# Expert weights in 4 MB transfers: four rows dealt per partition, and one place fewer ahead

## The chip, the cores and the metric

The kernel runs on one core of a Trainium2 chip. The metric is the device time of one execution in microseconds (us). The kernel before takes 1209.77 us, the median of 3 runs (1209.13 to 1209.91).

## What is computed

One layer of a hybrid decoder for 288 tokens (256 of a prompt, 8 x 4 of samples, width 1024, everything in float32). The front part is a projection of the normalised input into four parts, a gated linear recurrence and a pooling branch, a merge, and an output projection with a residual. The part that matters here is the mixture of 32 experts behind it, of which every token uses 4:

```python
def moe(u, w_router, b_router, w_gate_up, b_gate_up, w_down, b_down):
...
    for e in range(N_EXPERTS):
        gu = t @ w_gate_up[e] + b_gate_up[e]
        gate = jnp.minimum(gu[:, :D_EXPERT], SWIGLU_LIMIT)
        up = jnp.clip(gu[:, D_EXPERT:], -SWIGLU_LIMIT, SWIGLU_LIMIT)
        h = (up + 1.0) * (gate * jax.nn.sigmoid(SWIGLU_ALPHA * gate))
        out = out + comb[:, e:e + 1] * (h @ w_down[e] + b_down[e])
```

`w_gate_up[e]` is 1024 x 2048 and `w_down[e]` 1024 x 1024, so an expert has 12 MB (12,582,912 bytes) of weights, and the 32 experts 403 MB, each read once. A tail follows: the embedding of the layer, gated by a projection with `w_ple_gate` (4 MB), and a last norm.

## The kernel before

**Pieces.** The weights of an expert come in six pieces of 2 MB: four of gate and up (`w_gate_up`), each of 256 channels (rows of the matrix), and two of `w_down`, each of 512 rows. A piece lies over 128 partitions with 16 KB in each. For gate and up partition p holds the rows 2p and 2p+1 of its 256 (`k=2` in `expert_piece`, L661), 8 KB each and neighbours in memory; for down it holds the rows 4p to 4p+3 of its 512. So each partition is one run of 16 KB. In SBUF a piece is four blocks of 1024 values.

**Order.** Experts go in pairs, m = 0 to 15, and pairs in quads of 24 pieces (`STREAM`, L94). Within a pair the order is: gate and up of the even expert (4 pieces), of the odd one (4), down of the even one (2), of the odd one (2). Pieces are numbered 0 to 191 here.

**Places.** The ring has eight places (`SLOTS`), in which pieces follow one another. Beside them are two extra places, made of buffers that other stages have left. `AHEAD = {8: 0, 9: 1, 18: 1, 27: 1, 36: 1}` says which pieces lie in one of these: piece 8 in the first, and 9, 18, 27 and 36 one after another in the second, which is called the ninth place here. `held_before` (L132) tells which piece held the place of piece n before. An extra place is filled by two transfers, of 1.5 and 0.5 MB.

**SP** issues all weight transfers, in order: before each one it waits until the piece that held the place has been used (`opening_piece`, L694, for the first two quads; `quad_pieces`, L673, in a loop for five quads and once more for the last quad; `ring_place_used`, L655). Its transfers run one behind another on the same 16 DMA engines. The last piece comes as two halves, so that PE can start on the first. Behind it SP loads `w_ple_gate` in four transfers of 1 MB (L751), which need two ring places.

**PE** (`quad`, L1267) does for a pair: bias products for gate and up (`begin_sums`, L1178), 4 x 16 matmuls of 512 columns (`weigh_gate_up`, L1201), the sums of the pair before (`add_pair`, L1236), gate and up of the odd expert, the turned hidden rows (`turn_hidden`, L1168), down of both (`weigh_down`, L1222, 16 matmuls for each piece), and the gathered tokens of the next pair (`gather`, L1076 and L1083). Expert products have 64 token rows, and two of them run at once on two halves of the array: half g makes the output columns 512g to 512g+511. PE waits for a piece in `wait_expert_piece` (L494), and after its last matmul raises the semaphore on which SP waits.

**Tokens.** `x_tok` holds the normalised token rows in order. The gather reads them with a step of two (`x_blocks`, `"p (j c k) -> p j k c"`, k=2), so that the gathered channels lie as the rows of a gate-and-up piece do, and VectorE scales them by `gain_pairs` when it takes them (`gathered`, L2094).

**ScalarE** (`quad`, L1638) does the sigmoid, the copies out of PSUM, and, in pair 0, `copy_residual` (L1606), which copies two token tiles to where the sums are kept. **GpSimd** loads small things; `p_sample` (L817) goes into memory that the ninth place uses, so it waits until piece 36 is used.

## Time and profile before

| | |
|---|---|
| median of 3 runs | 1209.77 us (1209.13 to 1209.91) |
| profiled execution: time, span | 1210.05 us, 1208.3 us |
| PE busy | 1169.4 us (97%) |
| VectorE, ScalarE, GpSimd busy | 27%, 18%, 2% |
| mean granted TensorE clock | 0.996 |
| read from HBM | 444.51 MB, 369 GB/s over the span |
| SP's DMA queue | 440.04 MB in 50512 packets |

The span runs from the first instruction to the last one; the execution's own time is 1.75 us longer. PE's 97% is time in which some matmul was in flight, and that of the expert stage contains two at once. GB/s in a window of the page is what all 16 DMA engines moved. The page's slices are 30.2 us long.

### The profile page before, as it was taken

The page shows a single profiled execution, that of the slowest core. Times are in us where ns is not written, and L with a number is a line of the kernel's source. Part 1 is how long each engine was busy: PE and PEld are TensorE (multiplying, and loading weights), DVE is VectorE, ACT ScalarE, POOL GpSimd, SP SyncE. Part 2 cuts the span into 40 slices and gives each one's busy share as a digit, 9 for nine tenths or more (in the row PEclk, how much of TensorE's full clock was granted, in tenths as well). Part 3 has the DMA queues.
Part 4 walks back from the last instruction along what each step waited for, and adds up shares of the span by engine and source line. Part 5 has one row for each costly group of instructions (what it writes and reads, how often), then busy time and mean ns, then how long its engine had stood idle before and what let it go on. Part 6 is the DMA issues. An engine that isn't in the chain of part 4 may idle for free.

```text
span 1208.3 us, 14638 instructions
## 1 busy us (share of the span) xinstructions
PE 1169.4 (97%) x5836; PEld 553.0 (46%) x5836; DVE 331.4 (27%) x864; ACT 213.7 (18%) x420; POOL 29.2 (2%) x64
## 2 busy tenths in 40 slices
PE   9999999999999999999989899999998999799997
PEld 7777777443443434343333333434434343334344
DVE  4844214250322222131312120313222212111223
ACT  2556302112010101101010112120101010101034
POOL 2001000000000000000000020000000000000000
PEclk9999999999999999999999999999999999999999
DMA  9935573679999999999999999999999999999961
GB/s 287 360 141 203 173 279 133 237 283 429 427 428 426 427 426 428 427 427 429 427 428 428 427 428 425 429 427 426 430 426 428 427 428 430 425 428 428 426 260 40
DMA packets 53287, 446.82 MB, mean 370 GB/s; under 512 B 8174, under 2 KB 11470, under 8 KB 28424
## 3 DMA queue, kind: packets, MB, share of 16 engines
q1 hardware_dynamic: 50512, 440.04, 87.8%
q0 software_dynamic: 2464, 5.71, 1.6%
q8 instruction: 40, 0.66, 0.2%
q10 hardware_dynamic: 256, 0.30, 0.1%
q14 instruction: 15, 0.12, 0.0%
HBM read 444.51 MB, written 1.88 MB: 369 GB/s over the span
## 4 chain that ended last, share of the span: by engine, by line
PE 78%; DMA 20%; ACT 1%; DVE 1%; issue 1%; SPq 0%; DVEq 0%
PE ps L1201 31%; PE ps L864 16%; DMA ring<-in_w_gate_up 14%; PE ps L1222 11%; PE ps L1236 4%; PE ps L1083 3%; DMA ring<-in_w_down 3%; DMA ring<-in_w_ple_gate 2%; PE ps L1016 2%; PE ps L1355 2%; PE ps L1178 2%; PE ps L1168 1%; PE ps L898 1%; PE ps L858 1%; PE ps L885 1%; PE ps L1076 1%
## 5 line engine op out<-in xcount | busy, mean ns | idle before, releaser
L1201 PE MATMUL ps<-ring,work 128*64 128x512 f32 x2000 | 443.6, 597 | 2.8 <-DMA ring<-in_w_gate_up 2.6
L1201 PEld LDWEIGHTS ps<-ring,work 128*64 128x64 f32 x2000 | 141.2, 138 | 273.6 <-issue 261.9
L1222 PE MATMUL ps<-ring,work 128*64 128x512 f32 x992 | 223.4, 595 | 19.4 <-DMA ring<-in_w_down 19.4
L864 PE MATMUL ps<-work,ring 128*128 128x288 f32 x736 | 180.6, 407 | 0.0
L864 PEld LDWEIGHTS ps<-work,ring 128*128 128x128 f32 x736 | 139.7, 190 | 39.6 <-issue 1.7
L1222 PEld LDWEIGHTS ps<-ring,work 128*64 128x64 f32 x992 | 70.6, 137 | 146.8 <-issue 127.6
L2122 DVE TENSOR_SCALAR work<-ps 128x512 f32<-128x512 f32 x32 | 22.1, 691 | 374.5 <-PE ps L1201 374.5
L2094 DVE TENSOR_TENSOR work<-ps,gain_pairs 128x256 f32<-128x256 f32 x60 | 25.5, 424 | 286.2 <-PE ps L1083 286.2
L1626 ACT ACTIVATE work<-work 128x512 f32<-128x512 f32 x32 | 20.2, 631 | 442.9 <-DVE work L2122 442.9
L1083 PE MATMUL ps<-work,x_tok 128*128 128x128 f32 x512 | 65.4, 285 | 0.0
L1083 PEld LDWEIGHTS ps<-work,x_tok 128*128 128x128 f32 x512 | 61.8, 197 | 3.9 <-issue 2.0
L1236 PE MATMUL ps<-work 128*128 128x512 f32 x128 | 59.2, 606 | 1.4 <-DVE stat L1944 1.4
L1570 ACT COPY work<-ps 128x512 f32<-128x512 f32 x32 | 18.7, 585 | 196.1 <-PE ps L1168 196.1
L1635 ACT COPY work<-ps 64x512 f32<-64x512 f32 x31 | 17.9, 578 | 152.5 <-PE ps L1222 152.5
L2105 DVE TENSOR_TENSOR u_tok<-u_tok,ps 128x512 f32<-128x512 f32 x64 | 40.8, 680 | 2.5 <-PE ps L1236 2.5
L1236 PEld LDWEIGHTS ps<-work 128*128 128x128 f32 x128 | 23.0, 190 | 31.0 <-issue 29.1
L1168 PEld LDWEIGHTS ps<-ident,work 128*128 128x128 f32 x128 | 17.9, 209 | 26.0 <-issue 26.0
L1016 PE MATMUL ps<-ring,work 128*128 128x512 f32 x64 | 28.9, 600 | 0.0
L1355 PE MATMUL ps<-ring 128*128 128x512 f32 (+1 forms) x80 | 28.3, 511 | 0.3 <-DMA ring<-in_w_ple_gate 0.3
L1178 PE MATMUL ps<-work,pick_gu 96*64 96x512 bf16 x128 | 20.6, 399 | 4.8 <-issue 4.4
L1168 PE MATMUL ps<-ident,work 128*128 128x128 f32 x128 | 23.9, 310 | 0.0
L2124 DVE TENSOR_SCALAR work<-ps 128x512 f32<-128x512 f32 x32 | 22.1, 691 | 5.3 <-PE ps L1201 5.3
(286 smaller groups left out, 663.0 us busy)
## 6 DMA issues: line engine op xcount, KB each, us to landing
ring<-in_w_gate_up SPq DMA_DIRECT2D x125, 2048.0 KB, 29.5
ring<-in_w_down SPq DMA_DIRECT2D x61, 2048.0 KB, 29.6
ring<-in_w_in SPq DMA_DIRECT2D x7, 2048.0 KB, 19.0
work<-in_w_gate_up SPq DMA_DIRECT2D x3, 1536.0 KB, 12.9
ring<-in_w_proj_b SPq DMA_DIRECT2D x2, 2048.0 KB, 10.0
ring<-in_w_proj_a SPq DMA_DIRECT2D x2, 2048.0 KB, 10.1
ring<-in_w_out SPq DMA_DIRECT2D x2, 2048.0 KB, 9.4
ring<-in_w_ple_gate SPq DMA_DIRECT2D x4, 1024.0 KB, 28.6
```

Source lines behind the costliest of these rows:

```text
L864: mm = pe.matmul(out(b), lhs, rhs, start=(k == 0), stop=(k == len(pairs) - 1))
L1016: mm = pe.matmul(ps[0:ROWS[t], b, :], out_rows[t][k], out_weights[half][k], start=(k == 0), stop=(k == KC - 1))
L1083: mm = pe.matmul(ps[:, B_X[q], k * P:k * P + P], x_blocks[t][:, q, k, :], sel[t], start=False, stop=(last and k == 1))
L1168: mm = pe.transpose(ps[:, b, j * P:j * P + P], block, ident[:])
L1178: pe.matmul(ps[half(g), b, :], pick[0:BIAS_ROWS, :], bias_parts[0:BIAS_ROWS, at + 512 * g:at + 512 * g + 512], start=True, stop=False)
L1201: mm = pe.matmul(ps[half(g), b, :], xg[:, k, i % 2, :], blocks[2 * (k % 2) + at][:, 512 * g:512 * g + 512], start=False, stop=(k == KC - 1))
L1222: mm = pe.matmul(ps[half(g), b, :], hT_of[i % 2][:, 4 * j + k, :], blocks[k][:, 512 * g:512 * g + 512], start=False, stop=(4 * j + k == KC ...
L1236: mm = pe.matmul(ps[:, bank, :], sel_wT[:, t, :], o_pair[:, 512 * h:512 * h + 512], start=True, stop=True)
L1355: mm = pe.matmul(ps[:, b, 0:c1 - c0], x2T[:, k, tok(t)], gate_rows(k, c0, c1), start=(k == 0), stop=(k == KC - 1))
L2094: V.tensor_tensor(xg[:, own, :, :], ps[:, b, 0:2 * P].rearrange("p (c i s) -> p c i s", c=2, i=2), gains, ALU.mult).then_inc(emptied[b], 1)
L2105: V.tensor_tensor(x_half, x_half, ps[:, bank, 0:own.stop - own.start], ALU.add) \
L2122: V.tensor_scalar(gate, ps[:, b, :], LIMIT, None, ALU.min).then_inc(emptied[b], 1)
```

## The change

It has five parts.

1. From piece 20 on (`JOINED = 20`), SP joins two pieces that follow one another in `STREAM` (two of gate and up, or the two of down) into one transfer of 4 MB, which fills two ring places. Its source is 512 rows of gate and up, four to a partition (`RUN = 4`), or all 1024 rows of down, eight to a partition: one run of 32 KB each. It is issued when the second of the two places is free. PE waits for both pieces on one semaphore. Pieces 0 to 19 stay transfers of 2 MB. The last two pieces (190, 191) also stay apart, and 191 stays in halves. That makes 85 transfers of 4 MB.
2. `AHEAD` becomes `{8: 0, 9: 1}`: the ninth place holds piece 9 alone, and 18, 27 and 36 go into the ring. The ring then turns in pairs of places.
3. Gate and up rows lie in fours from pair 2 on, so the gathered channels have to as well. ScalarE rewrites the token tiles once, in pair 1 (`deal_inputs`): two copies of 128 x 1024 and eight small ones of 32 x 128. From pair 2 on the gather reads these rows, now without a step, and the gains come from a second table (`gain_fours`), which GpSimd loads.
4. Down rows lie in eights. So half g of the array now makes the output columns 8c+4g to 8c+4g+3 of gate and up, for all c: each gate and up matmul, and its bias product, reads its moving operand as 128 groups of four values with a step of eight (`dealt`), where it read 512 values in a row. This holds for all pairs.
5. GpSimd no longer waits for piece 36 before it loads `p_sample`.

```diff
+RUN = 4
+
+JOINED = 20
+
+DEALT_PARTS = 10
...
-AHEAD = {8: 0, 9: 1, 18: 1, 27: 1, 36: 1}
+AHEAD = {8: 0, 9: 1}
...
+        def two_pieces(q):
+
+            return ring[:, MOE_SLOT[q]:MOE_SLOT[q] + 2, :, :].rearrange("p s a b -> p (s a b)")
+
+        def dealt(row, g):
+
+            return row.rearrange("p (c g k) -> p c g k", g=2, k=RUN)[:, :, g, :]
+
+        def in_fours(m):
+
+            return not (isinstance(m, int) and m < 2)
...
-            eng.wait_ge(piece_landed[s], turn * 16 + 16)
+            at = STREAM.index((i, q))
+            first, turn = (s, turn) if isinstance(Q, int) and Q * QUAD_PIECES + at < JOINED else \
+                place(Q, *STREAM[at // 2 * 2])
+            eng.wait_ge(piece_landed[first], turn * 16 + 16)
...
-            def expert_piece(r, q, e, in_halves=False):
+            def expert_rows(q, e):
 
                 if q < GU_PIECES:
-                    src = gu_rows[bass.ds(e * D + 2 * P * q, 2 * P), :].rearrange("(p k) c -> p (k c)", k=2)
-                else:
-                    src = dn_rows[bass.ds(e * D + 4 * P * (q - GU_PIECES), 4 * P), :] \
-                        .rearrange("(p k) c -> p (k c)", k=4)
-                if in_halves:
-                    sp.dma_start(whole_piece(r)[:, 0:2 * D], src[:, 0:2 * D]).then_inc(last_half_landed, 16)
-                    sp.dma_start(whole_piece(r)[:, 2 * D:4 * D], src[:, 2 * D:4 * D]).then_inc(piece_landed[r], 16)
-                    return
-                sp.dma_start(whole_piece(r), src).then_inc(piece_landed[r], 16)
+                    return gu_rows[bass.ds(e * D + RUN * P * (q // 2), RUN * P), :] \
+                        .rearrange("(p k) c -> p (k c)", k=RUN)
+                return dn_rows[bass.ds(e * D, D), :].rearrange("(p k) c -> p (k c)", k=2 * RUN)
+
+            def piece_half(q):
+
+                return slice(RUN * D * (q % 2), RUN * D * (q % 2) + RUN * D)
 
             def quad_pieces(quads, e0, last=False):
 
-                for at in range(QUAD_PIECES):
-                    ring_place_used(quads, at)
+                for at in range(0, QUAD_PIECES, 2):
                     i, q = STREAM[at]
-                    expert_piece((at - EXTRAS) % SLOTS, q, e0 + i, last and at == QUAD_PIECES - 1)
+                    r = (at - EXTRAS) % SLOTS
+                    if last and at == QUAD_PIECES - 2:
+                        ring_place_used(quads, at)
+                        sp.dma_start(whole_piece(r), expert_rows(q, e0 + i)[:, piece_half(q)]) \
+                            .then_inc(piece_landed[r], 16)
+                        ring_place_used(quads, at + 1)
+                        place_, src = whole_piece((r + 1) % SLOTS), expert_rows(q + 1, e0 + i)[:, piece_half(q + 1)]
+                        sp.dma_start(place_[:, 0:2 * D], src[:, 0:2 * D]).then_inc(last_half_landed, 16)
+                        sp.dma_start(place_[:, 2 * D:4 * D], src[:, 2 * D:4 * D]).then_inc(last_landed, 16)
+                        continue
+                    ring_place_used(quads, at + 1)
+                    sp.dma_start(two_pieces(r), expert_rows(q, e0 + i)).then_inc(piece_landed[r], 16)
...
             def opening_piece(n):
 
-                later, at = divmod(held_before(n), QUAD_PIECES)
+                later, at = divmod(held_before(n if n < JOINED else n + 1), QUAD_PIECES)
                 i, q = STREAM[at]
                 piece_used(i, q, later)
-                if n in AHEAD:
-                    three, one = extra_parts[AHEAD[n]]
-                    extra_rows(n, 0, three)
-                    extra_rows(n, 3, one)
+                r = ring_turn(n) % SLOTS
+                if n < JOINED:
+                    sp.dma_start(whole_piece(r), piece_rows(n)).then_inc(piece_landed[r], 16)
                     return
                 later, at = divmod(n, QUAD_PIECES)
                 i, q = STREAM[at]
-                expert_piece(ring_turn(n) % SLOTS, q, 4 * later + i)
+                sp.dma_start(two_pieces(r), expert_rows(q, 4 * later + i)).then_inc(piece_landed[r], 16)
...
-            for n in range(SLOTS + 2, OPENING * QUAD_PIECES):
+            for n in list(range(SLOTS + EXTRAS, JOINED)) + list(range(JOINED, OPENING * QUAD_PIECES, 2)):
...
-            quads, at = divmod(max(AHEAD), QUAD_PIECES)
-            i, q = STREAM[at]
-            pool.wait_ge(piece_used_up[q], 4 * quads + i + 1)
...
+            x_fours = [x_tok[:, t, :].rearrange("p (j k c) -> p j k c", c=P, k=2) for t in range(TT - 1)]
...
-                gather_samples()
+                if isinstance(m, int) and m == 2:
+                    pe.wait_ge(x1_dealt, DEALT_PARTS)
+                gather_samples(in_fours(m))
                 for q in range(QUARTERS):
                     for t in TILES[1:]:
-                        gather_tile(q, t)
+                        gather_tile(q, t, in_fours(m))
...
+                    row = bias_parts[0:BIAS_ROWS, at:at + D]
                     pe.matmul(ps[half(g), b, :], pick[0:BIAS_ROWS, :],
-                              bias_parts[0:BIAS_ROWS, at + 512 * g:at + 512 * g + 512],
+                              row[:, 512 * g:512 * g + 512] if kind == "out" else dealt(row, g),
...
                             mm = pe.matmul(ps[half(g), b, :], xg[:, k, i % 2, :],
-                                           blocks[2 * (k % 2) + at][:, 512 * g:512 * g + 512],
+                                           dealt(blocks[2 * (k % 2) + at], g),
...
+            def deal_inputs():
+
+                for b in B_X:
+                    act.wait_ge(filled[b], inputs_gathered(b, 1, False))
+                for t in range(2):
+                    act.wait_ge(x1_copied, t + 1)
+                    nc.scalar.copy(x_tok[:, t, :].rearrange("p (j k c) -> p j k c", k=RUN, c=P),
+                                   x2[t].rearrange("p (j c k) -> p j k c", k=RUN, c=P)).then_inc(x1_dealt, 1)
+                act.wait_ge(comb_ready, 1)
+                src = flat_x[:, 2 * D:2 * D + QW].rearrange("p (c g k) -> p g k c", g=2, k=2)
+                for j in range(2):
+                    for g in range(2):
+                        for h in range(2):
+                            nc.scalar.copy(sample_fours[own_quarter(2 * j + g), :, 64 * h:64 * h + 64],
+                                           src[own_quarter(2 * j + h), g, :, :]).then_inc(x1_dealt, 1)
```

**How it moves the instructions.** SP, the transfers behind pieces 8 and 9; the first row is pieces 10 and 11. Before (L671 is the ring, L692 the ninth place):

```order
L671 DMA ring<-in_w_down 128x4096 x2
L671 DMA ring<-in_w_gate_up 128x4096 x6
L692 DMA work<-in_w_gate_up 128x3072
L692 DMA work<-in_w_gate_up 128x1024
L671 DMA ring<-in_w_gate_up 128x4096
L671 DMA ring<-in_w_down 128x4096 x4
L671 DMA ring<-in_w_gate_up 128x4096 x3
L692 DMA work<-in_w_gate_up 128x3072
L692 DMA work<-in_w_gate_up 128x1024
L671 DMA ring<-in_w_gate_up 128x4096 x4
```

And now (L748 is a transfer of 2 MB, L752 one of 4 MB; 4096 and 8192 are values per partition):

```order
L748 DMA ring<-in_w_down 128x4096 x2
L748 DMA ring<-in_w_gate_up 128x4096 x8
L752 DMA ring<-in_w_down 128x8192 x2
L752 DMA ring<-in_w_gate_up 128x8192 x4
L752 DMA ring<-in_w_down 128x8192 x2
L752 DMA ring<-in_w_gate_up 128x8192 x4
L752 DMA ring<-in_w_down 128x8192 x2
```

Before, the pieces 18, 27 and 36 went to the ninth place in two transfers each. Now 18 is the last but one of the single transfers, and from piece 20 on each transfer carries two pieces.

SP, the end of the program. Before (L668 and L669 are the halves of piece 191, L751 is `w_ple_gate`):

```order
L671 DMA ring<-in_w_down 128x4096 x3
L537 ISA
L668 DMA ring<-in_w_down 128x2048
L669 DMA ring<-in_w_down 128x2048
L652 ISA
L751 DMA ring<-in_w_ple_gate 128x2x1024 x4
```

And now (L703 is piece 190, L707 and L708 are the halves of 191):

```order
L711 DMA ring<-in_w_down 128x8192
L703 DMA ring<-in_w_down 128x4096
L562 ISA
L707 DMA ring<-in_w_down 128x2048
L708 DMA ring<-in_w_down 128x2048
L677 ISA
L781 DMA ring<-in_w_ple_gate 128x2x1024 x4
```

Pieces 188 and 189 were transfers of their own and are one now (L711); 190 and the halves of 191 stay.

ScalarE, the end of pair 0 and the begin of pair 1, now (L1641 is `copy_residual`, L1649 and L1656 are `deal_inputs`, L1677 is the sigmoid of pair 1):

```order
L1641 COPY u_tok<-x_tok 128x1024 x2
L1686 COPY work<-ps 64x512
L1687 COPY work<-ps 64x512
L1649 COPY x_tok<-u_tok 128x1024 x2
L1656 COPY x_tok<-x_tok 32x2x64 x8
L1677 ACTIVATE work<-work 128x512
```

Before, the sigmoid followed the two copies of `keep_output` (now L1686, L1687) at once.

## Rows read from the trace of the kernel before

**Rows 1.** The page, 40 slices of the span: DMA busy tenths and rate.

```profile
DMA  9935573679999999999999999999999999999961
GB/s 287 360 141 203 173 279 133 237 283 429 427 428 426 427 426 428 427 427 429 427 428 428 427 428 425 429 427 426 430 426 428 427 428 430 425 428 428 426 260 40
```

**Rows 2.** Windows, two stretches: busy us of each engine, granted clock, DMA share, GB/s.

```profile
core 0: us, PE busy (x) PEld busy (x) DVE busy (x) ACT busy (x) POOL busy (x), PEclk, DMA share, GB/s
60.00:70.00 10.00, 10.00 (x45) 7.29 (x44) 0.48 (x1) 8.22 (x18) 0.00 (x0) 1.00 1.05 387
400.00:500.00 100.00, 100.00 (x524) 39.82 (x522) 23.56 (x63) 9.24 (x16) 0.51 (x1) 1.00 1.01 427
```

**Rows 3.** DMA, 60 to 70 us: packets; issues with KB each and us to landing.

```profile
DMA packets 1919, 3.87 MB, mean 387 GB/s; under 512 B 31, under 2 KB 31, under 8 KB 1919
...
ring<-in_w_proj_b SPq DMA_DIRECT2D x1, 2048.0 KB, 12.2
```

**Rows 4.** DMA, 400 to 500 us, the same columns.

```profile
DMA packets 2957, 42.67 MB, mean 427 GB/s; under 512 B 339, under 2 KB 339, under 8 KB 355
...
ring<-in_w_gate_up SPq DMA_DIRECT2D x13, 2048.0 KB, 23.8
```

**Rows 5.** The chain that ended last: start us, us, what.

```profile
355.18 3.97 PE ps L1083 x32
359.69 13.73 PE ps L1201 x64
...
413.55 13.73 PE ps L1201 x64
...
554.50 32.79 DMA ring<-in_w_gate_up
...
669.51 35.27 DMA ring<-in_w_gate_up
...
1168.86 14.02 PE ps L1355 x32
```

**Rows 6.** Waits of the whole span, PE: us in total, times, longest.

```profile
PE ps L1222 <- DMA ring<-in_w_down: 19.4, 24, 1.2
...
PEld ps L1222 <- DMA ring<-in_w_down: 16.6, 13, 2.0
```

**Rows 7.** Timeline of SP: start us, us, transfers x count, pieces 19 to 23.

```profile
297.25 0.33 SPq L671 DMA_DIRECT2D ring<-in_w_gate_up  x1
300.68 15.83 SPq L671 DMA_DIRECT2D ring<-in_w_down  x4
```

**Rows 8.** Timeline of SP, one row: piece 22.

```profile
312.75 0.33 SPq L671 DMA_DIRECT2D ring<-in_w_down  x1
```

**Rows 9.** DMA, the one transfer issued at 297.25: us to landing.

```profile
ring<-in_w_gate_up SPq DMA_DIRECT2D x1, 2048.0 KB, 13.7
```

**Rows 10.** Source line L671, all 2 MB transfers: us from issue to landing.

```profile
DMA to landing us min/median/max: 7.7/29.6/36.1
```

**Rows 11.** Timeline of PE at the end of pair 15: start us, us, what [idle before].

```profile
1143.57 3.65 PE L1222 MATMUL ps<-ring,work 128*64 128x512 f32 x16 [0.40 <-DMA ring<-in_w_down]
...
1148.37 3.65 PE L1222 MATMUL ps<-ring,work 128*64 128x512 f32 x16 [0.47 <-DMA ring<-in_w_down]
...
1153.94 7.09 PE L1222 MATMUL ps<-ring,work 128*64 128x512 f32 x32 [1.10 <-DMA ring<-in_w_down]
...
1168.13 0.38 PE L904 MATMUL ps<-stat,fold 128*128 128x1 f32 x2
1168.86 6.71 PE L1355 MATMUL ps<-ring 128*128 128x512 f32 x15 [0.34 <-DMA ring<-in_w_ple_gate]
```

**Rows 12.** Groups of weight loads by form, whole span: busy us, mean ns.

```profile
L1083 PEld LDWEIGHTS ps<-work,x_tok 128*128 128x128 f32 x512 | 61.8, 197 | 3.9 <-issue 2.0
L1236 PEld LDWEIGHTS ps<-work 128*128 128x128 f32 x128 | 23.0, 190 | 31.0 <-issue 29.1 <-DVE stat L1944 1.9
L1168 PEld LDWEIGHTS ps<-ident,work 128*128 128x128 f32 x128 | 17.9, 209 | 26.0 <-issue 26.0
```

**Rows 13.** Groups of PE, pair 2 (359.53 to 413.38 us): busy us, mean ns.

```profile
L1201 PE MATMUL ps<-ring,work 128*64 128x512 f32 x112 | 24.6, 593 | 0.0
```

**Rows 14.** Timeline of ScalarE around pair 1.

```profile
294.57 1.99 ACT L1606 COPY u_tok<-x_tok 128x1024 f32<-128x1024 f32 x2
...
301.27 0.58 ACT L1636 COPY work<-ps 64x512 f32<-64x512 f32 x1
319.49 0.63 ACT L1626 ACTIVATE work<-work 128x512 f32<-128x512 f32 x1 [17.64 <-DVE work L2122]
```

**Rows 15.** Timeline of PE: the gather for pair 1.

```profile
301.25 4.04 PE L1083 MATMUL ps<-work,x_tok 128*128 128x128 f32 x32
```

**Rows 16.** Timeline of GpSimd: start us, us, what [idle before].

```profile
116.97 0.79 POOL L806 DMA_DIRECT2D gain_pairs<-in_g_moe  x1
130.61 0.51 POOL L810 DMA_DIRECT2D u_tok<-in_b_gate_up  x1 [12.85 <-ACT work L1458]
```

More of the change, by code:

```diff
@@ L435, in hybrid_layer @@
         x1_copied = sem("x1_copied")
+        x1_dealt = sem("x1_dealt")
         sel_w_ready = sem("sel_w_ready")
@@ L684, in piece_rows @@
                 e = 4 * quads + i
-                if q < GU_PIECES:
+                if q < GU_PIECES and not in_fours(n // (QUAD_PIECES // 2)):
                     return w_gate_up[0, e, 2 * P * q:2 * P * q + 2 * P, :].rearrange("(p k) c -> p (k c)", k=2)
-                rows = 4 * P * (q - GU_PIECES)
-                return w_down[0, e, rows:rows + 4 * P, :].rearrange("(p k) c -> p (k c)", k=4)
+                return expert_rows(q, e)[:, piece_half(q)]
             def extra_rows(n, k, dst):
@@ L807, in _ @@
                            g_moe[0].rearrange("(j p k) -> p j k", p=P, k=2)).then_inc(gain_landed, 16)
+            pool.dma_start(gain_fours[:].rearrange("p (j k) -> p j k", k=RUN),
+                           g_moe[0].rearrange("(j p k) -> p j k", p=P, k=RUN)).then_inc(gain_landed, 16)
             pool.wait_ge(ya_ready, PG)
@@ L1067, in _, with gather_samples @@
             turn_residual(1, 0)
-            x_blocks = [x_tok[:, t, :].rearrange("p (j c k) -> p j k c", c=P, k=2) for t in range(TT - 1)]
-            def gather_samples():
+            x_pairs = [x_tok[:, t, :].rearrange("p (j c k) -> p j k c", c=P, k=2) for t in range(TT - 1)]
+            x_fours = [x_tok[:, t, :].rearrange("p (j k c) -> p j k c", c=P, k=2) for t in range(TT - 1)]
+            def gather_samples(fours=False):
+                rows = sample_fours if fours else sample_rows
                 for k in range(2):
@@ L1075, in gather_samples, with gather_tile @@
                         own = own_quarter(q)
-                        pe.matmul(ps[:, b, k * P:k * P + P], sample_rows[own, k, :], sel[TT - 1][own, :],
+                        pe.matmul(ps[:, b, k * P:k * P + P], rows[own, k, :], sel[TT - 1][own, :],
                                   start=(k == 0), stop=False)
-            def gather_tile(q, t):
+            def gather_tile(q, t, fours=False):
                 last = t == TILES[-1]
+                x_blocks = x_fours if fours else x_pairs
                 for k in range(2):
@@ L1643, in quad @@
                         embedding_squares()
+                    if begins and j == 1:
+                        deal_inputs()
                     swish(m, 0)
@@ L2048, in _ @@
             b = turns["rank"][0]
-            dve.wait_ge(gain_landed, 16)
+            dve.wait_ge(gain_landed, 16 * 2)
             def take_inputs(q):
@@ L2092, in gathered @@
                     own = slice(2 * j, 2 * j + 2)
-                    gains = gain_pairs[:, own].unsqueeze(2).unsqueeze(3).to_broadcast([P, 2, 2, CAP])
+                    gains = (gain_fours if in_fours(m) else gain_pairs)[:, own].unsqueeze(2).unsqueeze(3) \
+                        .to_broadcast([P, 2, 2, CAP])
                     V.tensor_tensor(xg[:, own, :, :], ps[:, b, 0:2 * P].rearrange("p (c i s) -> p c i s", c=2, i=2), gains,
@@ L2158, in quad @@
                             dve.wait_ge(x1_copied, 2)
+                            dve.wait_ge(x1_dealt, 2)
                             dve.wait_ge(row_copied, 1)
```

10 lines of the change are left out of this document (6 added, 4 removed).

## The prediction

> **What bounds the kernel now.** I read the 40 slices first. From the tenth slice to the 38th the DMA engines are full and move 425 to 430 GB/s [rows 1]. Before it, in the front part, they are not full, so nothing that the change does there counts. Next I compared what the two sides need for one pair of experts. PE started gate and up of one pair at 359.69 us and of the next at 413.55, with no wait between: 53.86 us [rows 5]. A pair has 12 pieces, 25.17 MB, and at 427 GB/s [rows 2] that is 58.9 us. So DMA is the slower side by 5 us in a pair. PE begins with pieces in stock, and from about 554 us on it waits: the chain of waits then runs through transfers of weights (32.79 us at once at 554.50, 35.27 at 669.51) [rows 5], and PE waited for down pieces 19.4 and 16.6 us in total [rows 6]. These 36 us are all that PE has to spare. Last comes the end. PE waited 0.40, 0.47 and 1.10 us for pieces 188, 189 and 190, then 0.34 us for the last quarter of `w_ple_gate`, and began the last projection at 1168.86 [rows 11]. So two rules hold. A microsecond of the DMA stream after about 260 us is a microsecond of the kernel, whether it is a faster run or an idle queue. And at the very end PE is only 0.34 us from being the last itself.
>
> **The change, part by part.**
>
> *Longer runs, gain.* The cost of a run comes from two stretches with full engines. At 60 to 70 us the runs are of 2 KB (512 columns of a matrix; 1919 packets for 3.87 MB) and the rate is 387 GB/s; at 400 to 500 us they are of 16 KB and it is 427 [rows 2 to 4]. An engine has a sixteenth of that: 84.7 ns for 2048 B, 613.9 ns for 16384 B. The line through both is 36.9 ns for each 1000 bytes and 9.1 ns fixed per run. A run of 32 KB then takes 1218.6 ns instead of 1227.8. A 4 MB transfer has 8 such runs on each engine, which saves 8 x 9.1 = 73 ns, and there is one completion packet fewer per engine (339 small packets in 100 us are about 16 for each of 20 transfers [rows 4]), taken at the same 9 ns. Together 82 ns, and with 85 transfers 7.0 us. Bounds: the line could be steeper at its foot, or a run of 32 KB could be cut in two. Then only the completions are saved, 0.8 us. On the other side the rate cannot exceed the line's slope, 433.5 GB/s, which is 146 ns per transfer or 12.4 us. I take 7.0, since the straight line is all that the two rows support.
>
> The Trainium skill (SBUF — State Buffer, "The DMA setup-cost knee") has 2 us fixed per transfer and 436 GB/s behind it, so 4 MB in one would take 2 us less than in two, 170 us in all. The trace disagrees for transfers that queue: those of 2 MB already move at 427 GB/s.
>
> *The ninth place and the joined wait, loss.* This is what decides. In the trace before, SP issued piece 19 at 297.25, 20 at 300.68, 21, 22 and 23 behind it, with 22 at 312.75 [rows 7, 8]. Each time is the moment when PE had used the piece that held the place (9 for 18, 10 for 19, 11 for 20, 12 for 21, 13 for 22). Without the refill of the ninth place everything moves back by one: 18 takes the place of 10 (297.25), 19 that of 11 (300.68), 20 that of 12 and 21 that of 13. And 20 and 21 are the first joined transfer, so both wait for piece 13, until 312.75. The stock in the queue doesn't last so long. Piece 19 was issued at 297.25 and landed 13.7 us later, at 310.9 [rows 9]; it lands then in the change too, as 18 and 19 are still issued before the engines run dry (each piece takes 4.9 us). In an empty queue a transfer of 2 MB takes at least 7.7 us from issue to landing [rows 10], 2.8 us over its 4.9. So the first byte of 20 effectively flows at 315.5, where it would have followed at 310.9: the DMA engines idle for 4.6 us, or about 5.8 if the start of an empty queue takes as much as a typical one of that stretch. I take 5.0. Once is enough: 22 and 23 wait for piece 15 and 24 and 25 for 17, both freed in time, and after that PE, with 53.86 us a pair, frees places faster than DMA fills them. Nothing gives those 5.0 us back, since the engines are full from there to the end.
>
> *No refills of the ninth place.* Three refills came as two transfers with runs of 12 and 4 KB: per engine 8 runs and a completion more, 82 ns, times three. Gain 0.25 us.
>
> Up to here the stream is shifted by 5.0 - 0.25 - 7.0 = -2.25 us at its end.
>
> *Waiting for both pieces.* In the middle this costs nothing, for PE uses two pieces in 7 to 9 us and a landing comes every 9.7. At the end it does. Before, 188 could start at 1143.57, while 189 landed for 1148.37 [rows 11]. Now both start when 189 has landed, at 1148.37 - 2.25 = 1146.1. From the start of 188 to that of 189 PE needs 4.80 - 0.47 = 4.33 us, and from there to 190 5.57 - 1.10 = 4.47 [rows 11]. So 190 starts at 1154.9, not 1153.94: 1.0 us later, although the stream is earlier. PE is ready for the last projection at 1168.51 + 1.0 = 1169.5, `w_ple_gate` has landed at 1168.86 - 2.25 = 1166.6, and PE becomes the last: 1169.5 against 1168.86 is **+0.65 us**.
>
> *Dealt reads on PE.* No row shows a moving operand with a step. The nearest are weight loads of 128 x 128: 190 ns in a row, 197 ns at every second value, 209 ns at every fourth [rows 12]. The lower end is 0 (or a gain, if a row in pieces were quicker; nothing suggests it). The upper end takes the 19 ns of 128 values that each open a new 16 bytes: a matmul reads 128 groups, so +19 ns on 593 [rows 13], 3%, and up to four times that if each value suffers as in a weight load. I take 0, because a group of four float32 fills 16 bytes, and the reads in a row open a new 16 bytes as often.
>
> The rule behind this is in the Trainium skill (SBUF — State Buffer, "Door 1: The DMA port swizzle"): SBUF has lines of 16 bytes and going to a new one costs. By it the dealt read costs nothing. The weight loads above agree in direction; no row here shows the dealt read itself.
>
> *ScalarE's dealing.* Two copies like those of L1606 (1.99 us) and eight small ones, 4 us in all. They start when pair 1's tokens are gathered, at 305.3 [rows 15], and ScalarE's next work is at 319.49 [rows 14]: hidden. The first reader of the dealt rows is the gather at 355.18 [rows 5]. The gather itself then loads without a step, 190 instead of 197 ns; PE has the spare time anyway, 0. GpSimd's added load stands ahead of the bias loads, where GpSimd waits 12.85 us for other work and one load takes it 0.8 us [rows 16]: 0. Its dropped wait frees only a small load that nobody waits for: 0.
>
> **Sum.** 1210.05 + 0.65 = 1210.7 us for the profiled execution. The median of the runs is 0.28 less, so **1210.4 us**: no change. About 0.2%, 2.4 us, is what a measurement can tell from none.
>
> **Rivals.**
>
> *A. Dealt reads slow PE.* For: the weight loads do pay for a step. Against: 16 bytes stay together. Gate and up are eight pieces of 3.43 us in a pair (13.73 for four [rows 5]), 27.5 us. At +10% a pair needs 2.75 us more, 16 pairs 44 us, which is 8 over the 36 that PE has to spare: 1218. It decides from some 4% on, as the spare time isn't spread evenly, and at 5% it is about +3: 1213. Slower. Chance 0.15.
>
> *B. The change doesn't do what it says: a 32 KB run goes as two packets.* Then the shift is 5.0 - 0.25 - 0.8 = +3.95, 190 starts at 1148.37 + 3.95 + 8.8 = 1161.1, and the end is +6.9: 1216.6. Nothing in the trace has such a run, for or against. Chance 0.07.
>
> *C. The rate rises more than the line says.* At the line's slope, 433.5 GB/s, 12.4 us instead of 7.0: shift -7.65, and 190 starts at 1149.5, the end is -4.8: 1205.0. For: part of the fixed cost may belong to the transfer, not to the run. Against: the line. Chance 0.10. Chance 0.12. The Trainium skill (DMA: Bandwidth & Descriptors, "Where 436 GB/s comes from") has 435 GB/s as the ceiling; at that the saving would be 15.4 us and the time 1202.
>
> *D. The queue doesn't run dry at 310.9*, because PE frees 13 earlier: 5.0 us less, 1205.4. Against: PE was never waiting there, so it has nothing to be earlier by. Chance 0.03.
>
> *E. Something else costs PE a few us near the end,* where it has just become the last: longer packets ahead of its code, a lower granted clock after longer waits. +1 to +4, say 1212.5. Chance 0.09.
>
> The forecast itself has 0.56. Its own range is 1208.6 to 1213.2: the saving between 5 and 8.6 us, the idle queue between 4.6 and 5.8.
>
> **Numbers.** Faster: C and D, 0.13. Slower: B 0.07, most of A 0.12, most of E 0.07, together 0.26. The rest, 0.61, is the same. The range goes up to take in B and ends at 1216.8; it leaves out C and D (0.13) and the far end of A (0.05), and begins at 1206.5, which takes in a C of half the size.
>
> **What the new profile would show.** The rate in the windows from 400 us on: 430 to 431 GB/s (427: B, 433: C), with some 1,300 packets over 8 KB in 100 us instead of 2,602. A gap in DMA at about 309 to 315, with SP's first 128x8192 issue at 312.75. Gate and up matmuls at 593 ns and 13.73 us for 64 (more: A). At the end a wait of PE for pieces 188 and 189 together, none for `w_ple_gate`. I am wrong if the gap isn't there, or if the rate lies outside 429 to 432.

## The result, and the profile after

The changed kernel takes **1228.14 us** (median of 4 runs, 1227.73 to 1228.84) beside 1209.45 us (4 runs, 1209.13 to 1209.91) for the kernel before: a ratio of 1.0156, 95% interval 1.0144 to 1.0168. It is 18.7 us slower. The forecast was 1210.4 us, in a range that ended at 1216.8. (Where a line number in the text above differs by a few lines from the printed listing, the listing is right. Below, line numbers are those of each kernel's own file.)

The page of the changed kernel, profiled at 1228.20 us:

```profile
span 1226.5 us, 14434 instructions
...
PE   9999999999999999998989996799999999799997
...
DMA  9936563589899999999999999599999999999951
GB/s 288 374 115 223 183 272 132 223 331 420 362 427 430 432 434 428 429 432 431 433 430 433 431 432 430 230 396 437 431 427 431 434 433 430 430 431 431 423 215 39
DMA packets 40647, 446.82 MB, mean 364 GB/s; under 512 B 6798, under 2 KB 10094, under 8 KB 26664
...
q1 hardware_dynamic: 37840, 440.03, 85.9%
```

Beside the same row for the kernel before [rows 1] one sees three things. The rate in the full stretches went from 427 to some 431 GB/s. The 11th slice, at 307 to 337 us, is at 362. And the 26th slice, at 767 to 797 us, is at 230. Nothing in the prediction speaks of that last one. Windows of the changed kernel around the places:

```profile
core 0: us, PE busy (x) PEld busy (x) DVE busy (x) ACT busy (x) POOL busy (x), PEclk, DMA share, GB/s
...
300.00:320.00 20.00, 20.00 (x126) 9.50 (x127) 6.40 (x22) 8.94 (x13) 0.00 (x0) 1.00 0.79 325
...
400.00:500.00 100.00, 99.52 (x522) 38.95 (x520) 24.55 (x65) 9.77 (x17) 0.00 (x0) 1.00 1.00 431
```

```profile
755.00:760.00 5.00, 0.00 (x0) 0.00 (x0) 0.00 (x0) 0.00 (x0) 0.00 (x0) 0.67 0.98 419
...
770.00:775.00 5.00, 1.55 (x16) 0.60 (x16) 0.00 (x0) 2.05 (x4) 0.00 (x0) 0.50 0.40 173
775.00:780.00 5.00, 5.00 (x24) 1.64 (x22) 0.00 (x0) 0.37 (x1) 0.00 (x0) 0.79 0.00 0
780.00:785.00 5.00, 5.00 (x42) 2.32 (x39) 0.00 (x0) 1.44 (x3) 0.00 (x0) 1.00 0.29 79
```

First PE stands still with all engines (755 to 760), while DMA works on. Then the DMA engines run dry (770 to 785). The chain that ended last says who holds whom:

```profile
719.39 2.02 ACT work L1617 x4
721.41 0.65 ACT tails L1620 x3
722.06 0.09 issue
722.15 9.67 POOL out L862 x19
731.82 40.98 DMA out<-work
772.79 0.02 issue
772.82 0.59 ACT work L1600
773.41 0.04 issue
773.45 1.94 PE ps L927 x16
```

The 40.98 us are neither weights nor any transfer that the change touches. GpSimd issues 20 stores of the recurrent state (16 of `conv_sample` and `pool_sample`, and four more) in pair 8. The tile `ple`, into which ScalarE next copies the embedding (`keep_embedding`, L1589 before), lies on the memory of that state (`state_z`), so ScalarE waits until all stores have landed. PE waits for ScalarE, frees no ring place, SP cannot issue, and the queue runs dry. The same places before and now, first the kernel before (timelines of GpSimd and ScalarE; issues with KB each and us to landing):

```profile
717.56 10.19 POOL L833 DMA_DIRECT2D out<-work  x20 [299.76 <-ACT tails L1585]
...
747.26 1.56 ACT L1565 COPY work<-ps 128x512 f32<-128x512 f32 x3 [3.19 <-DMA out<-work]
...
out<-work POOLq DMA_DIRECT2D x9, 12.0 KB, 12.0
out<-work POOLq DMA_DIRECT2D x8, 16.0 KB, 13.2
```

The changed kernel, with PE's wait and SP's four issues of this stretch (the last one is at 783.67, 39 us behind the third):

```profile
722.15 10.19 POOL L862 DMA_DIRECT2D out<-work  x20 [428.58 <-ACT tails L1620]
...
772.82 2.05 ACT L1600 COPY work<-ps 128x512 f32<-128x512 f32 x4 [24.14 <-DMA out<-work]
...
PE ps L927 <- ACT work L1600: 19.1, 1, 19.1
...
729.74 54.26 SPq L711 DMA_DIRECT2D ring<-in_w_gate_up  x4
...
out<-work POOLq DMA_DIRECT2D x9, 12.0 KB, 24.7
out<-work POOLq DMA_DIRECT2D x8, 16.0 KB, 27.6
```

The stores take GpSimd the same 10.19 us to issue, and twice as long to land: 24.7 and 27.6 us instead of 12.0 and 13.2. ScalarE waited 3.19 us before and 24.14 now. PE waited 19.10 us, so its own work covered about 5.0 of ScalarE's 24.14. By that estimate the chain was, before, only some 1.8 us (5.0 - 3.19) short of showing on PE.

Why twice as long? The stores are 640 packets on GpSimd's queue in both kernels, 40 for each of the 16 engines; 542 of them have 4 bytes. Their packets (queue q0: count, MB, share of the 16 engines' time) in two stretches, 715 to 735 and 735 to 760 us, of the kernel before:

```profile
q0 software_dynamic: 384, 0.21, 3.5%
...
q0 software_dynamic: 256, 0.13, 1.7%
```

and the changed kernel, the same stretches (715 to 735, 735 to 760 us) and a third, 760 to 775:

```profile
q0 software_dynamic: 133, 0.11, 1.7%
...
q0 software_dynamic: 351, 0.16, 2.2%
...
q0 software_dynamic: 156, 0.07, 1.7%
```

The records of single packets name no engine, but the order shows in them: behind 573 of the 640 packets before, and 584 of the 640 now, a packet of weights starts within 5 ns of its end. I read that as turns: an engine does one packet of GpSimd's queue, then one of SP's, and so on. SP's packet was 16 KB and 0.61 us; now it is 32 KB and 1.22 us. 40 turns are 24.6 us before and 48.7 us now; in the records the 640 packets run from 721.2 to 746.8 us and from 725.9 to 772.4. The Trainium skill (DMA: Bandwidth & Descriptors, "Queues, rings and completion order") says that an engine takes turns between the rows of its queues, a packet at a time, with some 9 to 17 descriptors in a packet. The trace agrees on the turns; on SP's side a turn is here a single run of a partition, 16 or 32 KB, and its length is what the other queue pays.

**Where the 18.2 us are** (the difference of the two profiled spans). PE starts the last projection at 1187.03 us (1168.86 before [rows 11]). The bytes that SP's queue has moved by a time, in pieces of 2 MiB, split it (a piece takes 4.88 us):

| us | before | after | difference | in us | cause |
|---|---|---|---|---|---|
| 340 | 41.67 | 40.74 | -0.93 | -4.5 | idle queue at 310 |
| 720 | 119.00 | 118.78 | -0.22 | +3.5 | longer runs |
| 850 | 145.26 | 141.87 | -3.39 | -15.5 | the stores |
| 1150 | 206.34 | 203.43 | -2.91 | +2.3 | longer runs |

(The causes are assigned by what lies in each stretch; the experiments below try them one by one.) The stream is 14.2 us late at the end. The other 4.0 us are PE's, in the last pair (timeline of the changed kernel; before: [rows 11]):

```profile
1162.17 5.35 PE L1257 MATMUL ps<-ring,work 128*64 128x512 f32 x16 [2.51 <-DMA ring<-in_w_down]
...
1168.13 3.65 PE L1257 MATMUL ps<-ring,work 128*64 128x512 f32 x16
...
1172.44 7.03 PE L1257 MATMUL ps<-ring,work 128*64 128x512 f32 x32
...
1187.03 13.97 PE L1390 MATMUL ps<-ring 128*128 128x512 f32 x32
```

PE waits once, 2.51 us, for 188 and 189 together, and the 16 matmuls after it take 5.35 us instead of 3.65: the granted clock stood at half, 1.2 GHz, for 3.4 us from 1162.8 on. Before, it had waited 0.40 and 0.47 us there and kept the clock.

### The profile page after: what moved, and what is told of

It reads as the page before. It is cut to its first block, busy times and chain, and to the rows that moved or that the text cites. A ratio compares the mean times of both kernels' runs of the same rounds, so it can differ in the third digit from the quotient of the medians.

```text
span 1226.5 us, 14434 instructions
## 1 busy us (share of the span) xinstructions
PE 1167.6 (95%) x5836; PEld 550.9 (45%) x5836; DVE 331.5 (27%) x864; ACT 220.8 (18%) x430; POOL 29.9 (2%) x65
## 4 chain that ended last, share of the span: by engine, by line
PE 76%; DMA 21%; ACT 1%; DVE 1%; POOL 1%; issue 1%; SPq 0%; DVEq 0%; ACTq 0%
PE ps L1236 28%; PE ps L893 16%; PE ps L1257 13%; DMA ring<-in_w_down 10%; DMA ring<-in_w_gate_up 8%; PE ps L1115 4%; PE ps L1271 4%; DMA out<-work 3%; PE ps L1045 2%; PE ps L1390 2%; PE ps L1213 2%; PE ps L1202 1%; PE ps L927 1%; POOL out L862 1%; PE ps L1107 1%; PE ps L914 1%
## 5 line engine op out<-in xcount | busy, mean ns | idle before, releaser
L1236 PE MATMUL ps<-ring,work 128*64 128x512 f32 x2048 | 451.8, 595 | 3.4 <-DMA ring<-in_w_gate_up 3.3
L1236 PEld LDWEIGHTS ps<-ring,work 128*64 128x64 f32 x2048 | 145.2, 137 | 278.9 <-issue 265.8
L1257 PE MATMUL ps<-ring,work 128*64 128x512 f32 x992 | 226.1, 604 | 19.6 <-DMA ring<-in_w_down 19.6
L1257 PEld LDWEIGHTS ps<-ring,work 128*64 128x64 f32 x992 | 71.7, 139 | 148.2 <-issue 141.5
L2148 DVE TENSOR_TENSOR work<-ps,gain_fours 128x256 f32<-128x256 f32 x56 | 23.8, 425 | 286.8 <-PE ps L1115 286.8
L1677 ACT ACTIVATE work<-work 128x512 f32<-128x512 f32 x32 | 20.2, 631 | 428.1 <-DVE work L2176 428.1
L1115 PE MATMUL ps<-work,x_tok 128*128 128x128 f32 x512 | 62.6, 280 | 0.0
L1115 PEld LDWEIGHTS ps<-work,x_tok 128*128 128x128 f32 x512 | 59.0, 192 | 3.9 <-issue 2.1
L1605 ACT COPY work<-ps 128x512 f32<-128x512 f32 x32 | 18.7, 585 | 209.0 <-PE ps L1202 209.0
L1686 ACT COPY work<-ps 64x512 f32<-64x512 f32 x31 | 17.9, 578 | 143.8 <-PE ps L1257 143.8
L1213 PE MATMUL ps<-work,pick_gu 96*64 96x512 bf16 x128 | 21.2, 408 | 5.0 <-issue 4.7
```

The costliest lines, as they stand in the source:

```text
L1115: mm = pe.matmul(ps[:, B_X[q], k * P:k * P + P], x_blocks[t][:, q, k, :], sel[t], start=False, stop=(last and k == 1))
L1213: pe.matmul(ps[half(g), b, :], pick[0:BIAS_ROWS, :], row[:, 512 * g:512 * g + 512] if kind == "out" else dealt(row, g), start=True, stop=F ...
L1236: mm = pe.matmul(ps[half(g), b, :], xg[:, k, i % 2, :], dealt(blocks[2 * (k % 2) + at], g), start=False, stop=(k == KC - 1))
L1257: mm = pe.matmul(ps[half(g), b, :], hT_of[i % 2][:, 4 * j + k, :], blocks[k][:, 512 * g:512 * g + 512], start=False, stop=(4 * j + k == KC ...
L2148: V.tensor_tensor(xg[:, own, :, :], ps[:, b, 0:2 * P].rearrange("p (c i s) -> p c i s", c=2, i=2), gains, ALU.mult).then_inc(emptied[b], 1)
```

## The experiments

Theory S: small stores take turns with long packets, and this is the loss. Rivals: something else in the change holds pair 8 (the dealt rows, the joined waits), or the early gap and the tail weigh more than thought. Each ratio is to the kernel before in the same session (1209.42 to 1209.48 us).

**Runs of 16 KB, the rest of the change kept.**

```diff
-                    sp.dma_start(two_pieces(r), expert_rows(q, e0 + i)).then_inc(piece_landed[r], 16)
+                    both_pieces(r, expert_rows(q, e0 + i))
```

`both_pieces` issues the two halves of each partition's run as two transfers of 2 MB, one behind the other, at the same moment; PE still waits for both.

> The changed kernel, but each 4 MB transfer is issued as two of 2 MB right behind one another, with runs of 16 KB. Places, waits for places and PE's wait for both pieces stay. Theory (each small packet of the state stores on GpSimd's queue waits for one weight packet on its DMA engine, and these are twice as long now): the stores land some 26 us after the first issue instead of 50, PE's 19 us wait in the embedding and the idle DMA behind it go, and what stays is the idle queue at 309 us and the late end: 1216. The rate is back at 427 GB/s. Rival (the joined waits and the missing ninth place themselves make the embedding late): the wait stays, 1228.

Measured: 1219.14 us, ratio 1.0079 (1.0062 to 1.0095). The stall is gone: ScalarE waits for no store, and the stores land in 11.8 and 13.1 us. The rate is 427 GB/s again. But 3 us more are lost than expected: at 1150 us its stream is 0.94 pieces, 4.6 us, behind that of the kernel before, and its last projection starts 9.0 us later (1177.84), so 4.4 us lie in the last pair.

**Eleven stores instead of 20, the rest of the change kept.** The 16 stores of the samples go by row of the window instead of by sample:

```diff
-            for b in range(DB):
-                at = 16 + DS * b
-                stores += [(conv_sample[0, b], state_z[at + 1:at + DS, 0, :]),
-                           (pool_sample[0, b, PB - DS:PB, :], state_z[at:at + DS, 1, :])]
+            for i in range(DS):
+                own = slice(16 + i, 16 + DS * DB, DS)
+                stores += [(pool_sample[0, :, PB - DS + i, :], state_z[own, 1, :])]
+                if i:
+                    stores += [(conv_sample[0, :, i - 1, :], state_z[own, 0, :])]
```

> The changed kernel, but the 16 stores of sample state are made as 7, one for each token position over all 8 samples: 11 store transfers instead of 20 for the same bytes. Theory: 22 packets per engine instead of 40, at 1.2 us each about 27 us, the wait goes nearly whole: 1210 (my first forecast was 1210.4). Rival (it isn't the number of small packets; the bytes or the weight stream decide): 1228.

Measured: **1211.08 us**, ratio 1.0017 (1.0007 to 1.0027). This edit alone gives back 17.1 of the 18.7 us. Its trace has 352 packets for the stores, 22 per engine, and

```profile
722.25 5.60 POOL L863 DMA_DIRECT2D out<-work  x11 [428.60 <-ACT tails L1621]
...
752.45 1.56 ACT L1601 COPY work<-ps 128x512 f32<-128x512 f32 x3 [3.67 <-DMA out<-work]
```

with no wait of PE. (The profiled execution took 1213.71 us, near the top of its runs.)

**JOINED = 24**, four more pieces in transfers of their own.

> The changed kernel, but joined from piece 24 on (20 to 23 stay single, so 20 waits for piece 12 only). Theory: of the 4.2 us in which DMA idles at 309 us 3 go, all else stays: 1225. Rival (that gap is no loss, because the stall in the embedding covers it): 1228.

Measured: 1228.02 us, ratio 1.0150 (1.0133 to 1.0167): a miss. The gap at 310 shrinks (DMA share 0.93 from 300 to 320), but 24 and 25 now wait for piece 17, until 331.55, and a second gap opens there (0.89 from 320 to 340). At 340 us the stream stands at 40.74 pieces, as in the changed kernel: the gap was moved, not removed. So the prediction's "freed in time" for pieces 24 and 25 holds only behind a gap that has already been paid. The stall in pair 8 is there as in the changed kernel. As the gap stayed, the run doesn't decide its rival, that the gap costs nothing beside the stall.

**The kernel before with more stores**: each of its 16 sample stores in two, 36 transfers in all, weights in 16 KB runs.

```diff
+            stores = stores[:4] + [(dst[k], src[k]) for dst, src in stores[4:] for k in (slice(0, 2), slice(2, None))]
```

> The kernel before, with its runs of 16 KB, but each of the 16 stores of sample state is made as two: 36 store transfers instead of 20. Theory: 72 packets per engine instead of 40, each behind a weight packet of 0.61 us, so they land some 45 us after the first issue, as in the changed kernel: PE waits some 19 us in the embedding, and the time rises by 12 to 18 us to 1222 to 1228. Rival (the run length alone, or the joined waits, make the stall): 1209.5.

Measured: 1216.33 us, ratio 1.0059 (1.0042 to 1.0076). Nothing of the change is in this kernel, and it has the stall:

```profile
764.85 2.05 ACT L1566 COPY work<-ps 128x512 f32<-128x512 f32 x4 [20.84 <-DMA out<-work]
...
PE ps L899 <- ACT work L1566: 12.8, 1, 12.8
```

The time is less than expected (1222 to 1228): PE's wait was 12.8 us instead of 19.1, the DMA engines idled some 3.5 us, and the stream lost 6.8 us between 720 and 850 us instead of 15.5. That the ring refills here place by place, and in the changed kernel two places at a time, may have its part in this; no run shows it alone. The four kernels by one rule, packets per engine times SP's packet:

| kernel | store packets per engine | SP's packet | product | first store issued to ScalarE's copy |
|---|---|---|---|---|
| before | 40 | 0.61 us | 24.6 us | 29.7 us |
| seven stores | 22 | 1.22 us | 26.8 us | 30.2 us |
| before, stores halved | 72 | 0.61 us | 44.2 us | 47.7 us |
| changed | 40 | 1.22 us | 48.7 us | 50.7 us |

The product orders all four and leaves 2 to 5 us for the issue. With the three edits above (shorter packets or fewer stores take the stall away, more stores bring it into the kernel before), that settles S.

**What the rest of the change is worth.** With the seven stores: 188 and 189 apart again.

```diff
+                    if last and at == QUAD_PIECES - 4:
+                        for h, landed_ in enumerate((piece_landed[r], even_landed)):
+                            ring_place_used(quads, at + h)
+                            sp.dma_start(whole_piece(r + h), expert_rows(q, e0 + i)[:, piece_half(q + h)]) \
+                                .then_inc(landed_, 16)
+                        continue
```

> The changed kernel with 7 stores of sample state (the second experiment, 1211.1), and pieces 188 and 189 as transfers of their own. Theory (at the end PE waits 2.5 us for the joined 188 and 189, and behind that wait runs 3.4 us at half clock): both go, and since the weight stream of that run was 2.1 us ahead of that of the kernel before at 1150 us, the time is 1207.5. Rival (the end is set by the stream, not by the joined wait): 1211.

Measured: 1209.63 us, ratio 1.0000 (0.9991 to 1.0009), 1.4 us less than without the edit by the medians, 2.1 by the ratios (expected 3.6). In its profiled execution (1210.94 us) PE waits for no transfer from 1040 us on, so an earlier stream has nothing more to give there.

With the seven stores and JOINED = 36 (transfers of 4 MB from the second quad's middle on):

> The changed kernel with 7 stores, joined from piece 36 on. Theory (joining costs a gap where the queue's stock is short of one piece; at 36 the stock has grown enough, while from 24 the gap only moved to 330 us): no gap in DMA after 260 us, 4.5 us less than 1211.1: 1206.6. Rival (a gap comes at whatever piece joining begins): 1211.

Measured: 1209.56 us, ratio 0.9998 (0.9989 to 1.0007), 1.5 us less than with JOINED = 20, where 4.5 were expected. The DMA share from 300 to 320 us is 0.94, so a part of the gap is left.

With all three:

> Both edits together, with 7 stores: theory 1203, the longer runs' gain without the gap, the late end and the stall. If the gain of the runs were smaller than 7 us: 1206 or more.

Measured: **1207.0 us**, ratio 0.9976 (0.9967 to 0.9985). It beats both kernels, by 2.5 and 21 us, and is 4 us short of what was expected.

Two things explain the shortfall. The first, 1.8 us, is what the ninth place was worth, tried on the kernel before with `AHEAD = {8: 0, 9: 1}` and GpSimd's wait for piece 36 taken out, nothing joined:

> The kernel before, in which only the ninth place is filled once (pieces 18, 27 and 36 go into the ring), with nothing joined. Theory (the gap comes from the missing place and the joined wait together; alone the missing place delays piece 20 only until 309.3): a gap of about 1 us at 309 us, and the time is 1210.3. Rival (the missing place alone makes the gap of 4 to 5 us): 1213.5.

Measured: 1211.14 us, ratio 1.0016 (1.0007 to 1.0025), between the theory and its rival. SP issues 20 at 309.29, when the last parts of 19 are still landing, and yet the windows from 300 to 320 us, of the kernel before and of this one, read

```profile
300.00:320.00 20.00, 20.00 (x128) 9.19 (x124) 5.75 (x21) 1.67 (x3) 0.00 (x0) 1.00 1.01 426
```

```profile
300.00:320.00 20.00, 20.00 (x128) 9.19 (x124) 5.77 (x21) 1.70 (x3) 0.00 (x0) 1.00 0.96 385
```

The mean of 20 us hides where this is lost. The same execution in shorter windows:

```profile
309.00:310.00 1.00, 1.00 (x8) 0.34 (x6) 0.00 (x0) 0.00 (x0) 0.00 (x0) 1.00 0.29 115
310.00:311.00 1.00, 1.00 (x8) 0.36 (x6) 0.00 (x0) 0.00 (x0) 0.00 (x0) 1.00 1.29 262
311.00:312.00 1.00, 1.00 (x6) 0.28 (x4) 0.00 (x0) 0.00 (x0) 0.00 (x0) 1.00 0.58 197
305.00:309.00 4.00, 4.00 (x23) 1.46 (x23) 3.40 (x16) 0.00 (x0) 0.00 (x0) 1.00 1.00 422
```

From 305 to 309 us the rate is 422 GB/s (424 before), although piece 18 has landed by 306.8 and 19 is then alone in the queue. From 309 to 312 it is 191 instead of 426, which makes some 1.7 us: piece 20, issued as 19 ends, comes too late to follow without a gap. At 1150 us the stream is 0.37 pieces late, 1.8 us, and the kernel 1.7. In the kernels with JOINED = 36 the stream is 0.34 and 0.40 pieces late at 340 us, about the same.

The second is seen at the end of the 1207.0 us kernel (timeline of PE, to hold against [rows 11]):

```profile
1037.16 7.09 PE L1269 MATMUL ps<-ring,work 128*64 128x512 f32 x32 [0.98 <-DMA ring<-in_w_down]
...
1135.76 7.09 PE L1244 MATMUL ps<-ring,work 128*64 128x512 f32 x32 [0.38 <-DMA ring<-in_w_gate_up]
1142.89 3.60 PE L1269 MATMUL ps<-ring,work 128*64 128x512 f32 x16
...
1166.01 13.97 PE L1402 MATMUL ps<-ring 128*128 128x512 f32 x32
```

After 1037.16 PE waits 0.38 us for transfers in all. (One idle stretch of PE, 4.48 us before 1053.15, has no releaser in the profile; the kernel before has it too, 4.44 us before 1052.43.) The stream of this kernel is 0.91 pieces, 4.4 us, ahead of the kernel before at 1150 us, and the last projection starts only 2.85 us earlier: the bound has passed from DMA to PE, and the remaining 1.6 us buy nothing. With the 1.8 us that is 3.4 of the 4.

**What the long runs give.** The same kernel with runs of 16 KB:

```diff
-            eng.wait_ge(piece_landed[first], turn * 16 + 16)
+            eng.wait_ge(piece_landed[s], turn * 16 + 16)
...
-                    sp.dma_start(two_pieces(r), expert_rows(q, e0 + i)).then_inc(piece_landed[r], 16)
+                    both_pieces(r, expert_rows(q, e0 + i))
```

> The kernel with seven stores, 188 and 189 apart and JOINED = 36 (1207.0 us), with each 4 MB transfer issued as two of 2 MB with runs of 16 KB, at the same moment; each piece raises its own semaphore. Only the length of the runs differs. Theory (a run of 32 KB saves some 9 ns, about 82 ns per transfer): 75 of the transfers in the stream, 6.1 us later at the end of the stream. The 1207.0 us kernel has its stream 4.4 us ahead of the kernel before at 1150 us, but starts the last projection only 2.85 us earlier, so PE has 1.5 us in hand there: 1207.0 + 6.1 - 1.5 = 1211.6 us, and a rate of 427 instead of 431 GB/s. Rival (the stores and the end of the stream gave the 2.5 us, the runs nothing that counts): 1207. Stores: SPs packets of 16 KB let the small ones of the state land in 12 to 13 us at the median, with 32 KB it was longer.

Measured: 1211.29 us, ratio 1.0017 (1.0008 to 1.0026). By the ratios the runs alone are worth 0.41% of 1209.4, 5.0 us (4.4 by the medians; 1211.6 was expected); the stream is 1.11 pieces later at 1150 us, 5.4 us over 76 transfers, 71 ns each. The first two experiments differ by 1.37 pieces, 6.7 us over 85 transfers, 79 ns. It also shows theory S once more, on equal stores. Issues with KB each and us to landing, long runs first, then short:

```profile
out<-work POOLq DMA_DIRECT2D x8, 32.0 KB, 18.4
```

```profile
out<-work POOLq DMA_DIRECT2D x8, 32.0 KB, 10.0
```

**The kernel before with the eleven stores.**

> The kernel before with the 16 stores of the sample states made as 7 (11 transfers instead of 20), nothing else. Theory: ScalarE's wait of 3.19 us for these stores becomes short or none, and as PE never waited for it, the time stays: 1209.5, within 1 us. Rival (the seven stores are faster in themselves and the comparison of the changed kernels with them is coloured by that): 1207 or less, or 1212 or more.

Measured: 1209.97 us, ratio 1.0002 (0.9993 to 1.0011): no change. So the seven stores are no gain in themselves and mend only what the long packets spoil. Whether ScalarE's wait of 3.19 us went, as expected, is not shown: the one execution that was profiled took 6869.6 us, for a reason that stays open, and isn't used.

## Why the prediction was wrong, step by step

- **Which step failed.** The parts on ScalarE and GpSimd, "hidden" and "0", looked only at instructions that the change adds or drops there. No term asked what a packet of twice the length does to other transfers in flight on the same engines. That is the term of the sum that was missing, put at nothing: 15.5 us of stream, and 17.1 us of the kernel's time by the experiment with eleven stores. The row that would have given it stood in the trace before, ScalarE's 3.19 us of waiting for stores of the state. It says that the landing of these stores ends ScalarE's wait, and that anything which delays them delays ScalarE at once. Doubled packets add some 24 us by the product of the table above; ScalarE's wait grew by 21.0 us (3.19 to 24.14), PE's from nothing to 19.1.
- **The signs of being wrong** that the prediction named, no gap or a rate outside 429 to 432, did not come: the gap and the rate were as foretold. They tested only the terms on the list.
- **Rival E** had "longer packets ahead of its code" and "a lower granted clock after longer waits", with +1 to +4 us and a chance of 0.09. It was near the mechanism, in that longer packets hold up another queue, but the place and the size were not. The lower clock did come, at the end (below). No code was held up so far as the profile shows: PE's one long idle stretch without a releaser is 4.7 us in the changed kernel, and 4.4 before.
- **Longer runs**, -7.0 us, rate 430 to 431: right. 431 GB/s in 400 to 500 us, with 1,319 packets over 8 KB there (some 1,300 foretold), and 6.7 us by the first two experiments. B (427) and C (433) are out. (C stands with two chances, 0.10 and 0.12; the sums use 0.10.)
- **The ninth place and the joined wait**, +5.0 less 0.25: right. SP's first joined transfer left at 312.10 us (312.75 foretold), the DMA share from 300 to 320 is 0.79, and the stream has lost 4.5 us at 340. The experiment on the ninth place alone corrects its reason: 1.8 us are lost by the refill that is gone, even with nothing joined. "Once is enough" holds for JOINED = 20, but with JOINED = 24 the gap comes in two parts.
- **Waiting for both pieces**: the right mechanism, sized too small. Landing at 1146.1 and 190 at 1154.9 were foretold. Taken on the kernel with seven stores, where the stall doesn't shift it, PE started 188 at 1147.69, and 190 at 1157.95: 10.26 us later, where 8.8 was used. The clock at half after a wait of 2.5 us costs 1.7 us there, a little more than the whole difference of 1.5. This term was mis-sized. The last projection started at 1172.55, not 1169.5, in an execution 2.6 us above its kernel's median; over the runs, setting 188 and 189 apart gave 1.4 us.
- **Dealt reads**, 0: right, and A is out. The gate and up matmuls of the whole span and the gather, in the changed kernel:

```profile
L1236 PE MATMUL ps<-ring,work 128*64 128x512 f32 x2048 | 451.8, 595 | 3.4 <-DMA ring<-in_w_gate_up 3.3
...
L1115 PEld LDWEIGHTS ps<-work,x_tok 128*128 128x128 f32 x512 | 59.0, 192 | 3.9 <-issue 2.1
```

  595 ns a matmul, where it was 597; 64 of them 13.74 us, where it was 13.73 [rows 5]; and the gather's weight load 192 ns, where it was 197 [rows 12]. One dealt read did cost something, and it was not in the sum: the bias products of gate and up, in bf16, took 402 ns beside 392 before in the windows from 400 to 520 us, 0.6 us over the whole span (21.2 beside 20.6).
- **ScalarE's dealing**, 0: right. Its ten copies ran from 304.80 to 312.13 us, 7.4 us instead of the 4 that were reckoned, and were still done before 318.84, when its next work began.
- **The 36 us that PE has to spare** add the waits of PE to those of its weight loads, and both can stand before the same piece (at 567.8 us, 1.16 and 2.04 us). PE's own waits for pieces are 19.4 + 2.6 = 22.0 us. That changes only the price of rival A, which would have been higher.

With the stores mended, the kernel is at 1211.08 us, and the sum had said 1210.4. So what the sum counted came out within 1 us: the stream was 2.1 us ahead at 1150 us (2.25 foretold), and the end was mis-sized by 1.5. The sum failed by what it did not list. The chance for all that it had not listed was 0.09, and its price was taken from the last pair alone.

## What to carry to other kernels

When a change makes the packets of one DMA queue longer, list every transfer of the other queues that runs at the same time and count its packets per engine: each waits for one packet of the long queue, so packets times the time of one long packet is its new landing time (here with 2 to 5 us more for the issue). Then look who waits for it. A wait of a few us that stands there already, even on an engine with slack, is a warning: it shows that a later landing will be felt. Fewer, larger stores are the cheap cure, and how many 4 MB transfers are worth having ends where PE becomes the bound.

## What the runs showed of the hardware

- A small packet, most of them 4 bytes, cost its queue about the time of one packet of the other queue: 40 for each engine took 46.5 us beside packets of 32 KB (1.22 us each), and 25.6 us beside packets of 16 KB (0.61 us).
- The stores cost by their count: 640 packets for 20 transfers, 352 for 11, 1152 for 36, with the same 0.34 MB, that is 32 for each transfer. The Trainium skill (DMA: Bandwidth & Descriptors, "Why a DMA increments its semaphore by 16 and not by 1") has all 16 engines report for each transfer, however small. The counts fit and go beyond it: a report of each engine makes 16 packets for a transfer, and the count from 20 to 36 transfers rises by 512, 32 for each transfer more, at the same bytes. What the other 16 do, no run shows.
- A run of 32 KB was one packet, and took 71 to 79 ns less per 4 MB transfer than two of 16 KB.
- A queue whose next transfer was issued at 309.29 us, while the one before it was landing (308.8 to 311.5 us), moved 191 GB/s from 309 to 312 us instead of 426. From 305 to 309 us, for the most part with that one transfer alone, it moved 422.
- PE waited 2.51 us until 1162.17, and the granted clock stood at half, 1.2 GHz, for 3.4 us from 1162.8 on; PE waited 19.1 us until 773.45, and the clock stood at half from 756.7 to 777.1. At the end, where PE is the bound, that cost 1.7 us for 16 matmuls. What it cost in pair 8 is not shown by itself.
- Matmuls whose moving operand is 128 groups of four float32 with a step of eight took as long as those that read 512 in a row (595 and 597 ns). In bf16, where such a group has half the bytes, they took 402 ns beside 392.
